# The last block of a two-layer encoder kernel: rows of the prompt and of the sample in turn at two norms and one rounding

## The reference

```python
for layer in (0, 1):
    shift, scale, gate = split(c @ w_ada[layer] + b_ada[layer])
    h = rms_norm(x, norm_g[layer]) * (1 + scale) + shift
    if layer == 0:      # sliding-window attention and a state-space branch, side by side
        z = h @ w_in_even;  out = concat(o_a * silu(g_a), o_s * silu(g_s)) @ w_out_even
    else:               # gated short convolution
        b_g, c_g, hv, g_c = split(h @ w_in_odd)
        out = (silu(g_c) * b_g * short_conv(c_g * hv)) @ w_out_odd
    x = x + gate * out
y = rms_norm(x, final_g)
```

## Time and profile before

| what | value |
|---|---|
| time before, median of 3 runs | 2185.78 us (2183.31 to 2186.01) |
| the profiled execution: its own time | 2184.55 us |
| its span in the profile | 2182.8 us |
| mean granted clock of PE | 0.958 of full |
| busy: PE / DVE / ACT / POOL | 94% / 37% / 23% / 20% of the span |
| the chain that ended last, by engine | PE 87%, DVE 4%, DMA 3%, POOL 2%, issue 2%, ACT 1% |
| HBM traffic over the span | 188 GB/s |

### The profile page before, as it was taken

The page is one execution under the profiler, slowest core; times in us unless marked ns, Lnnn a source line. Parts: engine busy times, 40 slices in busy tenths (PEclk is TensorE's granted clock), DMA queues, the critical chain, the costliest instruction groups (busy, mean ns, idle before and its releaser), DMA issues.

```text
span 2182.8 us, 27958 instructions
## 1 busy us (share of the span) xinstructions
PE 2053.6 (94%) x11418; PEld 1638.3 (75%) x11434; DVE 801.2 (37%) x1502; ACT 496.6 (23%) x1047; POOL 442.2 (20%) x312
## 2 busy tenths in 40 slices
PE   8887899899999999999999999999999999799986
PEld 2256666688888857788887757888799876699986
DVE  7535272423443551312235543212425162322222
ACT  1232343322221431100121531000211442200010
POOL 0024514455431301001114001010104100100001
PEclk9988999999999999999999999999998999899998
DMA  8886735697778524555466414655474321345432
GB/s 283 309 240 231 263 152 172 242 316 273 259 291 264 188 87 173 193 189 188 175 198 243 173 62 169 233 191 187 156 235 148 127 78 69 125 155 175 176 145 72
DMA packets 86275, 415.00 MB, mean 190 GB/s; under 512 B 12404, under 2 KB 13460, under 8 KB 51892
## 3 DMA queue, kind: packets, MB, share of 16 engines
q1 hardware_dynamic: 79360, 396.37, 51.3%
q10 hardware_dynamic: 6788, 16.84, 2.6%
HBM read 323.51 MB, written 86.33 MB: 188 GB/s over the span
## 4 chain that ended last, share of the span: by engine, by line
PE 87%; DVE 4%; DMA 3%; POOL 2%; issue 2%; ACT 1%; SPq 0%; DVEq 0%; ACTq 0%; POOLq 0%
PE banks L762 17%; PE banks L760 17%; PE banks L761 17%; PE banks L789 16%; PE banks L1004 5%; PE banks L704 3%; PE banks L962 1%; PE banks L943 1%; PE banks L963 1%; PE banks L881 1%; PE banks L839 1%; DMA ring<-in_ada 1%; PE banks L869 1%; PE banks L812 1%; PE banks L822 1%
## 5 line engine op out<-in xcount | busy, mean ns | idle before, releaser
L760 PE MATMUL banks<-hh,pair 128*128 128x512 f32 x1464 | 584.5, 399 | 24.9 <-POOL pair L523 14.5
L762 PE MATMUL banks<-hh,pair 128*128 128x512 f32 x1464 | 584.8, 399 | 0.0
L761 PE MATMUL banks<-hl,pair 128*128 128x512 f32 x1464 | 577.4, 394 | 0.0
L789 PE MATMUL banks<-hh,pair 128*128 128x272 f32 x1952 | 332.9, 292 | 28.9 <-DVE hl L1604 12.7
L760 PEld LDWEIGHTS banks<-hh,pair 128*128 128x128 f32 x1464 | 278.8, 190 | 100.4 <-POOL pair L523 16.6
L761 PEld LDWEIGHTS banks<-hl,pair 128*128 128x128 f32 x1464 | 278.8, 190 | 68.0 <-issue 1.4
L762 PEld LDWEIGHTS banks<-hh,pair 128*128 128x128 f32 x1464 | 278.5, 190 | 61.5
L789 PEld LDWEIGHTS banks<-hh,pair 128*128 128x128 f32 x1952 | 282.4, 193 | 30.4 <-DVE hl L1604 12.8
L789 PE MATMUL banks<-hl,pair 128*128 128x272 f32 x976 | 205.1, 292 | 0.0
L523 POOL TENSOR_TENSOR pair<-ring,pair 128x1024 fp32r<-128x1024 f32 x62 | 152.8, 2467 | 209.2 <-ACT pair L514 209.2
L1339 POOL TENSOR_TENSOR pp_mem<-pp_mem 128x512 f32<-128x512 f32 x48 | 62.1, 1294 | 578.0 <-ACT pp_mem L1104 578.0
(11 more groups left out here) (294 smaller groups left out, 2300.2 us busy)
## 6 DMA issues: line engine op xcount, KB each, us to landing
pair<-parts_scratch SPq DMA_DIRECT2D x198, 1024.0 KB, 4.8
parts_scratch<-pair SPq DMA_DIRECT2D x66, 1024.0 KB, 7.7
ring<-in_dense SPq DMA_DIRECT2D x62, 512.0 KB, 5.2
pair<-ssm_scratch SPq DMA_DIRECT2D x24, 1024.0 KB, 7.5
ring<-in_ada SPq DMA_DIRECT2D x24, 512.0 KB, 4.7
p_H<-in_ada SPq DMA_DIRECT2D x24, 512.0 KB, 4.7
p_x<-in_x SPq DMA_DIRECT2D x4, 2048.0 KB, 24.7
pair<-glu_scratch SPq DMA_DIRECT2D x8, 1024.0 KB, 5.0
```

The lines of the kernel that those rows point to most:

```text
L760: pe.matmul(o, ah, bh, start=first, stop=False)
L761: pe.matmul(o, ah, bl, start=False, stop=False)
L762: return pe.matmul(o, al, bh, start=False, stop=last)
L789: mm = pe.matmul(o[n][:, WAT + WCOLS * half:WAT + WCOLS * (half + 1)], x, h[:, k, WCOLS * half:WCOLS * (half + 1)], start=(k == 0 and step ...
```

## The change

In the last block the three places go through the rows k in the outer loop and the streams in the inner one, so that the prompt's row k and the sample's row k follow each other: in ACT's `shift` of the second norm, in ACT's `round_mixed`, in DVE's `norms` (second norm and third norm's outputs) and in DVE's `split_mixed`. In blocks 1 to 3 there is one stream, and the order of the instructions is the same as before. No instruction is added or taken away; PE's, POOL's and SP's programs are the same. Each call keeps its waits.

```diff
@@ ACT, run_block @@
                 hi("hv0")
-                for S, b in streams(blk):
-                    shift(S, b, 1)
+                for k in range(KT):
+                    for S, b in streams(blk):
+                        shift(S, b, 1, (k,))
...
-                for S, b in streams(blk):
-                    for k in range(KT):
+                for k in range(KT):
+                    for S, b in streams(blk):
                         round_mixed(S, b, 1, k)
@@ DVE, norms @@
                 for S, b in streams:
                     diagonal(S, b, l)
-                for S, b in streams:
-                    for k in range(KT + 1):
+                for k in range(KT + 1):
+                    for S, b in streams:
                         if l < 2:
                             scale(S, b, l, k)
                         elif k < KT:
@@ DVE, run_block @@
                 if not last:
                     mean(prompt, blk, 0)
-                for S, b in streams(blk):
-                    split_mixed(S, b, 1, range(8))
+                for k in range(KT):
+                    for S, b in streams(blk):
+                        split_mixed(S, b, 1, (k,))
```

## The result

| | before | after |
|---|---|---|
| median, same chip | 2184.29 us (2182.71 to 2186.01, 5 runs) | 2170.83 us (2170.73 to 2173.76, 5 runs) |
| ratio of after to before | | 0.9948, 95% interval 0.9936 to 0.9960 |
| the profiled execution: own time, span | 2184.55, 2182.8 us | 2170.73, 2168.9 us |
| mean granted clock of PE | 0.958 | 0.960 |

By the medians the changed kernel is 13.5 us faster, by the ratio 11.4 us (8.7 to 14.0), as two of its five executions took 2173.5 and 2173.8 us. The forecast was 2171.5 us, in 2167.0 to 2175.0. Lines of the changed kernel stand one higher from L1266 on (L1604 of before is L1605).

The account below looks back on a forecast made before the run. PE, busy 94% of the span, was taken as the bound, losing time in two last-block waits. 2184.55 - 10.5 - 4.2 - 0.8 + 1.2 = 2170.3, plus 1.2 for the median: 2171.5 us, range 2167.0 to 2175.0.

Parts of the forecast that it names:

- What bounded PE: Last block: PE waited 12.7 us at the second norm and 7.0 at the rounding, behind all eight prompt rows.
- Second norm, start of PE: PE starts at 1896.65 instead of 1907.12, 10.5 us sooner, and doesn't run dry at DVE's 1.66 us a row.
- Rivals B and C: Second norm: hand-overs at 3.2 us a row give 2182.0 (0.04); PE fed slowly, 4.3 a row, about 2191 (0.02).
- rival D: Both restarts: PE then waits for something else, such as weights or a bank; about 2179 us, chance 0.06.
- Clock behind the norm: After the second norm's restart PE stays at half clock as long as now, 5.4 us: 0 gained.
- The bound's price: Behind the second norm, a half-clock stretch of 3.4 instead of 5.4 us would gain 1.0 us: half its shortening.
- Rounding, start of PE: Odd layer's rounding: PE starts 4.2 us sooner, POOL's product holding the sample's first rest; 5.2 without a hold.
- Clock at the rounding: Behind the rounding's wait, 3.4 us at half clock as in block 3, instead of 5.0: 0.8 us gained.
- The bound of "0.4 lost": Rounding, worst end: the clock stays low for 5.8 us, 0.4 us lost.
- rival A: Clock doesn't fall at the rounding and rises sooner at the norm: 1.7 to 2.7 us less, about 2169; chance 0.18.
- Third norm: End of kernel: the prompt's store goes out 1.1 us later, slowing later issues; 1.2 us lost (0.5 to 1.4).
- Sum: Whole kernel: 2184.55 - 10.5 - 4.2 - 0.8 + 1.2 = 2170.3; median 1.2 above, so 2171.5 us.

Follow-up runs that it names:

- turns of four: Kernel after, but the streams alternate every four rows at second norm and rounding, with the third norm by stream; 2172.60 us, ratio 0.9956 to before.
- kernel without the third norm: Kernel after, but the third norm's outputs go by stream as before; 2164.57 us, ratio 0.9917 to before.
- fillers at the norm: Third norm by stream, fillers at the rounding, plus throwaway PE matmuls in the last block's second norm (8 and 9); 2163.48 us, ratio 0.9915 to before.
- rounding alone: Kernel before, with only the odd layer's rounding and rests taking rows in turn; 2178.49 us, ratio 0.9977 to before.
- fillers at the rounding: Kernel after with the third norm by stream, plus 12 throwaway PE matmuls during the rounding wait; 2165.75 us, ratio 0.9922 to before.
- norm alone: Kernel before, with only the second norm taking its rows in turn; 2169.59 us, ratio 0.9939 to before.
- three rests early: Kernel after with the third norm by stream, and three rows of both streams' rests ahead of the last gate_b; 2166.84 us, ratio 0.9921 to before.

## Why the prediction was right, point by point

- **What bounded PE:** both waits were for the sample's first row behind eight prompt rows. Right, and the turns of four show it by dose: the norm's restart is at 2.8, 7.9 and 13.3 us with one, four and eight prompt rows ahead.
- **Second norm, start of PE:** 10.5 us forecast, 10.50 measured. The pace of DVE in turn, 1.66, is 1.64, and PE didn't run dry. Rivals B and C had 3.2 and 4.1 us a row. Nor did PE wait for anything new (rival D).
- **Clock behind the norm:** 0 forecast, +0.13 measured (5.7 us at half clock instead of 5.4). The bound's price, 0.5 us for a microsecond less of half clock, is near what the kernel without the third norm shows (1.24 us for 2.7 at first). It holds only while PE is behind DVE: with no half clock left at all, 5.7 us less, the fillers at the norm gained 1.65 us.
- **Rounding, start of PE:** 4.2 forecast, 4.28 measured; the hold of the sample's rest was there in the changed kernel and in the rounding alone, 1.26 us for 32 columns in both. The Trainium skill's rule (SBUF — State Buffer, section "Who interferes with whom"), that DVE instructions with two SBUF inputs and a reading GpSimd instruction exclude each other whatever their size, agrees: a rest of 32 columns takes 0.18 us with POOL idle and 1.26 to 1.33 where it waits for POOL's product to end.
- **Clock at the rounding: the step that was mis-sized.** The forecast had "1.7 us lost against 5.0/2 = 2.5 now, **0.8 us** gained"; it was 0.49 us lost, and this is most of the gap between the 14.3 us forecast and the 13.2 us that the change explains. It took the 3.4 us stretch of block 3 for the length of any such stretch; in the changed kernel it was 6.1 us. The price was a little off, too: against the 48.33 us from restart to last residual at full clock (fillers at the rounding), before lost 2.24 us for its 5.0 and the changed kernel 2.73 for its 6.1, so 0.45 a microsecond and not a half. The runs show 0, 3.4, 5.2 and 6.1 us of half clock behind the restart for waits of 2.7, 2.7, 7.0 and 2.7 us (rounding alone; without the third norm; norm alone; after). The bound of "0.4 lost" was just missed, rival A's kept clock did occur in the rounding alone, which has the same order there. The kernels that kept the clock show the whole term: 2.7 us of R.
- **Third norm:** 1.2 lost by forecast, 0.97 measured, 0.98 alone. The store moved by the 1.1 us forecast, and the sample's store was issued the forecast 0.5 us later; one more of the small issues was slowed, but only in part (0.74 for `v<-s_v`, 0.43 before).
- **Sum:** 14.3 less by forecast, 13.2 in the stages that the change explains, 13.8 in the profiled spans, 13.5 in the medians. That the time came within 0.7 us of the forecast is in part luck: 0.6 us came from stretches that the change doesn't touch, and the 1.2 us that the forecast adds for the median over the profiled execution were 0.1 in the changed kernel.
- **Range:** its ends are not what its terms give. With 2.5 us of scatter downwards the lower end would be 2164.6 instead of 2167.0, and the upper one 2173.6 instead of 2175.0. The measured time lies in both.

What stays open: the runs of the changed kernel fall into two groups, three near 2170.8 us and two near 2173.6. A kept or longer half-clock stretch would be of that size, but of the other executions only the mean granted clock is known (0.959 or 0.960 in all five), and 3.4 us of half clock would move it by 0.0008, so this was not shown. What decides whether the clock falls after a wait of 2.7 us is open as well. Nor was it tried what decides the turn when DVE's rests and POOL's product wait for each other; with three rests early POOL was the one that waited longest (3.23 us).

## What to carry to other kernels

Where a consumer needs one row of each of two streams to begin, the producer should take the streams in turn: the consumer's start moves by the rows that stood ahead, and with double buffers the turns cost nothing here. At the other end, where a large store waits for the last row of one stream, rows of a small second stream ahead of it only delay the store. Taking the third norm out of this change is worth 1 us. And where a product of POOL meets two-input DVE work on the path, enough of that work has to go ahead for the consumer's lead to cover the hold: one row moved it and won nothing, three rows won 1.1 us in the profile, which the timed runs could not confirm.

## What the runs showed of the hardware that was not expected

- The half clock at one and the same wait of 2.7 us cost nothing, 1.5 or 2.6 us in three kernels whose instructions around it were the same (rounding alone, without the third norm, after). Such a term has no single size; a forecast should carry it as a range.
- Where PE ran fillers in the wait at the rounding, the clock stayed full and R was 2.7 us shorter than in the changed kernel; but one kernel in three kept it without fillers, and the timed runs show no gain from these fillers alone. Ahead of the norm's restart the fillers went with a full clock at the restart and 1.65 us less behind it. At half clock a filler takes about twice as long (eight in 3.78 us, twelve in 2.94 at full clock), so their number has to fit the wait at the slow level, or they delay the work they are to speed up: eight in a wait of 1.9 us gave back 1.5 of the 1.65 us.
